# Quads two bodies earlier, indices decoded in PSUM, and the first value operands made inside the last key body

## The reference

```
q = (xb @ w_q).reshape(p, 8, 2, 128)
sc = jnp.einsum('thpc,hpnc->thpn', q, sub_keys)
s1, i1 = lax.top_k(sc[:, :, 0], 16);  s2, i2 = lax.top_k(sc[:, :, 1], 16)
cand = s1[..., :, None] + s2[..., None, :]
cand_idx = i1[..., :, None] * 128 + i2[..., None, :]
top_s, sel = lax.top_k(cand, 16)
eidx = take_along_axis(cand_idx, sel)
gate = softmax(top_s)
act = gelu(einsum('td,ted->te', xb, u[eidx])) * gate
out = einsum('te,ted->td', act, v[eidx])
```

## Time and profile before

| | |
|---|---|
| median of 3 runs | 2248.65 us (2247.8 to 2250.03) |
| profiled execution | 2248.29 us, span 2246.5 us |
| PE busy | 2128.1 us, 95% |
| DVE busy | 1473.0 us, 66% |
| ACT busy | 1312.9 us, 58% |
| POOL busy | 438.2 us, 20% |
| mean granted TensorE clock | 0.966 of 2.4 GHz |
| HBM | 336.66 MB read, 150 GB/s over the span |
| chain that ended last | PE 81%, DVE 8%, issue 4%, POOL 3%, ACT 2% |

### The profile page before, as it was taken

The page is one execution under the profiler, slowest core; times in us unless marked ns, Lnnn a source line. Parts: engine busy times, 40 slices in busy tenths (PEclk is TensorE's granted clock), DMA queues, the critical chain, the costliest instruction groups (busy, mean ns, idle before and its releaser), DMA issues.

```text
span 2246.5 us, 45241 instructions
## 1 busy us (share of the span) xinstructions
PE 2128.1 (95%) x14596; PEld 1927.4 (86%) x14596; DVE 1473.0 (66%) x2926; ACT 1312.9 (58%) x3097; POOL 438.2 (20%) x358
## 2 busy tenths in 40 slices
PE   7899899899999899999898998997999998999997
PEld 7889599899999788888787885997999997888886
DVE  5764247968878666666567533489687886666665
ACT  5530145479999755555564302553899996555554
POOL 0312007752222100000004020176522220000000
PEclk9999799999999999999999997998999999999999
DMA  5310244344444355555542102453444443555555
GB/s 222 113 57 1 94 150 171 144 153 168 157 161 168 131 187 194 198 187 192 182 183 94 57 1 94 169 176 124 169 165 155 166 158 141 189 195 194 188 196 186
DMA packets 47459, 338.77 MB, mean 151 GB/s; under 512 B 5648, under 2 KB 5776, under 8 KB 6928
## 3 DMA queue, kind: packets, MB, share of 16 engines
q1 hardware_dynamic: 47376, 337.73, 41.5%
HBM read 336.66 MB, written 1.05 MB: 150 GB/s over the span
## 4 chain that ended last, share of the span: by engine, by line
PE 81%; DVE 8%; issue 4%; POOL 3%; ACT 2%; DMA 2%; DVEq 0%; SPq 0%; POOLq 0%; PEldq 0%; ACTq 0%
PE ps L814 10%; PE ps L815 10%; PE ps L816 10%; PE ps L783 9%; PE ps L785 8%; PE ps L784 8%; POOL expert_lo L1826 3%; PE ps L686 3%; PE ps L407 2%; PE ps L409 2%; PE ps L408 2%; PE ps L550 2%; PE ps L563 1%; PE ps L562 1%; PE ps L793 1%
## 5 line engine op out<-in xcount | busy, mean ns | idle before, releaser
L783 PE MATMUL ps<-h_t_hi,expert_hi 128*128 128x256 f32 x2048 | 595.7, 291 | 27.3 <-DVE expert_lo L1656 22.1
L784 PE MATMUL ps<-h_t_lo,expert_hi 128*128 128x256 f32 x2048 | 582.8, 285 | 0.0
L785 PE MATMUL ps<-h_t_hi,expert_lo 128*128 128x256 f32 x2048 | 582.4, 284 | 0.0
L1826 POOL TENSOR_TENSOR expert_lo<-w_ring,expert_hi 128x512 fp32r<-128x512 f32 x220 | 338.1, 1544 | 763.9 <-ACT expert_hi L976 760.4
L783 PEld LDWEIGHTS ps<-h_t_hi,expert_hi 128*128 128x128 f32 x2048 | 396.0, 193 | 31.9 <-issue 13.3
L814 PE MATMUL ps<-expert_hi,act_hi 128*128 128x512 f32 x1024 | 400.5, 391 | 4.8 <-DVE act_lo L1664 4.8
L815 PE MATMUL ps<-expert_lo,act_hi 128*128 128x512 f32 x1024 | 400.1, 391 | 0.0
L816 PE MATMUL ps<-expert_hi,act_lo 128*128 128x512 f32 x1024 | 400.0, 391 | 0.0
L784 PEld LDWEIGHTS ps<-h_t_lo,expert_hi 128*128 128x128 f32 x2048 | 396.3, 194 | 0.0
L785 PEld LDWEIGHTS ps<-h_t_hi,expert_lo 128*128 128x128 f32 x2048 | 395.9, 193 | 0.0
L976 ACT CAST expert_hi<-w_ring 128x512 fp32r<-128x512 f32 x512 | 308.9, 615 | 141.9 <-PE ps L785 129.1
(11 more groups left out here) (293 smaller groups left out, 3359.5 us busy)
## 6 DMA issues: line engine op xcount, KB each, us to landing
w_ring<-u_t SPq DMA_DIRECT2D x128, 1024.0 KB, 4.8
w_ring<-v_t SPq DMA_DIRECT2D x128, 1024.0 KB, 4.8
w_ring<-w_in SPq DMA_DIRECT2D x32, 1024.0 KB, 4.9
w_ring<-w_q SPq DMA_DIRECT2D x16, 1024.0 KB, 4.9
w_ring<-w_out SPq DMA_DIRECT2D x8, 1024.0 KB, 4.8
big<-xconst SPq DMA_DIRECT2D x2, 1666.0 KB, 9.3
w_ring<-keys SPq DMA_DIRECT2D x2, 1024.0 KB, 4.8
big<-rows SPq DMA_DIRECT2D x2, 576.0 KB, 11.3
```

The lines of the kernel that those rows point to most:

```text
L783: pe.matmul(o, w_hi[:, c, :], HTH[:, d, :], start=d == 0, stop=False)
L784: pe.matmul(o, w_hi[:, c, :], HTL[:, d, :], start=False, stop=False)
L785: mm = pe.matmul(o, w_lo[:, c, :], HTH[:, d, :], start=False, stop=d == DC - 1)
L1826: pool.tensor_tensor(EL[:, m % 4, :], RING[:, m // 4, (m % 4) * 512:(m % 4 + 1) * 512], EH[:, m % 4, :].bitcast(F32), ALU.subtract).then_i ...
```

## The change

- QB goes from 12 to 10, FREE from 11 to 9 and EXP_BODY from 9 to 7. DVE has two lows a body in bodies 1 to 8, and the quads start in body 10. The slots of ones are made five a body in bodies 1 to 7.
- Body 30 has its three quads and prepares one more, body 31 has that one, and nothing stands between body 31 and the value product. In body 31 ACT and DVE make the first four splits of v and the first two of the activations where a body before makes those of the next body.
- The decode works on arrays of 16 x 16 for all 16 pairs of head and token tile at once. A key 128 x (start of the row in the table) + first index is picked by 15 comparisons and 15 predicated copies; from it come the first index (its low seven bits) and the column, which picks the second index in 15 more pairs. Positions and masks lie in PSUM banks 0 to 3 (DECODE), and a wait asks for all but the last instruction issued.
- Of 13 lows (17 before) that are threaded into the search some stand in other places.
- At the last level of `invert` the product with the upper half and its addition to TI are left out; nothing reads that half.

Cut to its core:

```diff
-N_BODY, EXP_BODY, FREE, QB = 32, 9, 11, 12
+N_BODY, EXP_BODY, FREE, QB = 32, 7, 9, 10
 N_QUAD = S // 4
-N_LOOPED = 3 * (N_BODY - QB)
+ONES = 5
...
+        DECODE = PS[:, 0:4, :].rearrange("p b n -> p (b n)").rearrange("p (m u n) -> p m u n", m=8, u=16)
...
-                            pe.matmul(PS[:, 4 + 2 * k, h * 64:(h + 1) * 64], TT[:, u, :], first, start=True, stop=True)
+                            if b < 64:
+                                pe.matmul(PS[:, 4 + 2 * k, h * 64:(h + 1) * 64], TT[:, u, :], first, start=True, stop=True)
...
-                with pe.Fori(QB, N_BODY) as j:
-                    u_and_quads(j)
-                for q in range(N_LOOPED, N_QUAD):
-                    quad(q % 3, q)
+                with pe.Fori(QB, N_BODY - 1) as j:
+                    u_and_quads(j, (1, 4, 6))
+                u_and_quads(N_BODY - 1, (1,))
...
                     if m < 8 or not last:
                         u_split(m % 8, j + m // 8, False)
+                    else:
+                        v_split(m - 8, 0, True)
+                        if m % 2 == 0:
+                            a_split((m - 8) // 2, 0, True)
...
                     if e == 0:
                         act.wait_ge(quad_out, 3 + N_QUAD)
+                else:
+                    if first and e == 2:
                         act.wait_ge(u_mul, 2 + 128 - LATE)
-                else:
                     act.wait_ge(v_done, 8 * j + 2 * e - 2)
...
-                    ones(bass.ds(LATE - 3 + 3 * j, 3), 3)
+                    ones(bass.ds(LATE - ONES + ONES * j, ONES), ONES)
...
-                for q in range(N_LOOPED + 2, N_QUAD):
-                    gate_rows(q % 3, q, 0, 8)
-                for m in range(4):
-                    v_split(m, 0, True)
-                for e in range(2):
-                    a_split(e, 0, True)
...
+                at = DECODE[:, 7, :, :]
+                dve.tensor_copy(PICK[:, :, :], ROWKEY[:, :, 0:1].broadcast_to([P, 16, 16]))
+                link(dve.tensor_copy(at, POS[:, :, :].bitcast(U32)))
...
+                def all_but(n):
+
+                    dve.wait_ge(dve_step, steps[0] - n)
+
+                def overwrite(dst, i, src):
+
+                    counted(dve.copy_predicated(dst[:, :, :], DECODE[:, i % 7, :, :].bitcast(U32), src.broadcast_to([P, 16, 16])))
+
+                for i in range(1, 17):
+                    if i < 16:
+                        counted(dve.tensor_scalar(DECODE[:, i % 7, :, :], at, float(ROW_AT[i]), None, ALU.is_ge))
+                    if i > 1:
+                        all_but(1 if i < 16 else 0)
+                        overwrite(PICK, i - 1, ROWKEY[:, :, i - 1:i])
+                    if i == 9:
+                        few_lows(1)
...
+                for i in range(1, 17):
+                    if i < 16:
+                        counted(dve.tensor_scalar(DECODE[:, i % 7, :, :], at, 128.0 * (i - 1), None, ALU.is_gt))
+                    if i > 1:
+                        all_but(1 if i < 16 else 0)
+                        overwrite(I2F, i - 1, x[:, :, 1, i - 1:i])
+                    if i in (6, 14):
+                        few_lows(1)
...
+                def next_lows(m):
+
+                    if not last:
+                        u_lows(m, j + 1)
+                    else:
+                        v_lows(m, 0)
+                        if m % 2 == 0:
+                            a_lows(m // 2, 0)
...
-                for q in range(N_LOOPED, N_QUAD):
-                    gated(q % 3, q, 128 - LATE)
-                    if q + 3 < N_QUAD:
-                        hots(q % 3, q + 3, False)
-                for m in range(2):
-                    v_lows(m, 0)
-                a_lows(0, 0)
-                for m in range(2, 8):
+                with dve.Fori(QB, N_BODY - 2) as j:
+                    u_and_gated(j, 3, 3, False)
+                u_and_gated(N_BODY - 2, 3, 1, False)
+                u_and_gated(N_BODY - 1, 1, 0, True)
+                for m in range(4, 8):
```

More of the change, by code:

```diff
@@ L795, in quad, with u_and_quads @@
                 mm.then_inc(quad_done, 1)
-            def u_and_quads(j):
-                q = 3 * (j - QB)
+            def u_and_quads(j, after):
                 for m in range(8):
                     u_half(m, j, False)
-                    if m in (1, 4, 6):
-                        i = (1, 4, 6).index(m)
-                        quad(i, q + i)
+                    if m in after:
+                        i = after.index(m)
+                        quad(i, 3 * (j - QB) + i)
             def v_half(m, j, first):
@@ L1011, in gate_rows, with u_and_gates @@
                     ins.then_inc(hot_gate, 1)
-            def u_and_gates(j, last):
+            def u_and_gates(j, quads, last):
                 q = 3 * (j - QB)
@@ L1023, in u_and_gates @@
                 u_gelu_late(0, j)
-                gate_rows(2, q + 2, 0, 6)
+                if quads:
+                    gate_rows(2, q + 2, 0, 6)
                 split(6)
@@ L1027, in u_and_gates @@
                 split(7)
-                gate_rows(2, q + 2, 6, 8)
-                gate_rows(0, q + 3, 0, 4)
+                if quads:
+                    gate_rows(2, q + 2, 6, 8)
+                    gate_rows(0, q + 3, 0, 4)
                 split(8)
@@ L1032, in u_and_gates @@
                 u_gelu_late(2, j)
-                gate_rows(0, q + 3, 4, 8)
-                gate_rows(1, q + 4, 0, 2)
+                if quads:
+                    gate_rows(0, q + 3, 4, 8)
+                if quads == 3:
+                    gate_rows(1, q + 4, 0, 2)
                 split(10)
@@ L1037, in u_and_gates @@
                 split(11)
-                gate_rows(1, q + 4, 2, 8)
+                if quads == 3:
+                    gate_rows(1, q + 4, 2, 8)
             def v_split(m, j, first):
@@ L1580, in topk @@
                         ins = dve.match_replace(SC2[:, u % 16, :], VAL[:, u, 0:8], SC[:, u, :], NEG)
-                        if u % 16 == (7 if t else 11):
+                        if t and u % 16 == 7:
                             few_lows(1)
@@ L1602, in topk @@
                     o += n
-                dve.tensor_copy(STEP1[:, :, 0:1], x[:, :, 0, 0:1])
-                dve.tensor_tensor(STEP1[:, :, 1:16], x[:, :, 0, 1:16], x[:, :, 0, 0:15], ALU.subtract)
+                rows = ROWC[:, 0, :].unsqueeze(1).broadcast_to([P, 16, 16])
+                dve.scalar_tensor_tensor(ROWKEY[:, :, :], rows, 128.0, x[:, :, 0, :], ALU.mult, ALU.add)
+                dve.tensor_copy(I2F[:, :, :], x[:, :, 1, 0:1].broadcast_to([P, 16, 16]))
                 link(dve.tensor_tensor(CAND[:, :, o:o + 8], v[:, :, 0, 8:16], v[:, :, 1, 0:1].broadcast_to([P, 16, 8]), ALU.add))
@@ L1685, in u_muls, with u_and_gated, quad_step, hot_step @@
                 dve.tensor_tensor(a, a, PS[:, 6 + e % 2, 0:S], ALU.mult).then_inc(u_mul, 1)
-            def u_and_gated(j, last):
+            def u_and_gated(j, quads, next_quads, last):
                 q, done = 3 * (j - QB), 4 * (j - QB)
+                def quad_step(i):
+                    if i < quads:
+                        gated(i, q + i, done + i)
+                def hot_step(i):
+                    if i < next_quads:
+                        hots(i, q + 3 + i, False)
+                def next_lows(m):
[5 more added lines that the diff above has]
+                            a_lows(m // 2, 0)
                 u_lows(4, j)
                 u_lows(5, j)
-                gated(0, q, done)
-                hots(0, q + 3, False)
+                quad_step(0)
+                hot_step(0)
                 u_lows(6, j)
-                u_muls(0, j, q + 1)
-                gated(1, q + 1, done + 1)
-                if not last:
-                    u_lows(0, j + 1)
-                hots(1, q + 4, False)
-                u_muls(1, j, q + 2)
-                if not last:
-                    u_lows(1, j + 1)
-                gated(2, q + 2, done + 2)
-                if not last:
-                    u_lows(2, j + 1)
-                hots(2, q + 5, False)
-                u_muls(2, j, q + 3)
-                u_muls(3, j, q + 3)
+                u_muls(0, j, q + min(1, quads))
+                quad_step(1)
+                next_lows(0)
+                hot_step(1)
+                u_muls(1, j, q + min(2, quads))
+                next_lows(1)
+                quad_step(2)
+                next_lows(2)
+                hot_step(2)
+                u_muls(2, j, q + quads)
+                if last:
+                    v_lows(3, 0)
+                u_muls(3, j, q + quads)
             norm_rows(0, HN)
```

71 lines of the change are left out of this document (33 added, 38 removed).

## The result

The changed kernel takes **2182.52 us** (median of 4 runs, 2180.91 to 2188.99) against 2248.70 for the kernel before: ratio 0.9711, 95% interval 0.9691 to 0.9731. The profiled execution took 2180.91 us, span 2179.1.

A forecast was written before the change was run, and what follows sets the result against it. PE, 95% busy, was taken as the bound, with VectorE bounding key bodies 5 to 9. Gain: 61.0 - 2 x 2.0 - 2 x 4.5 = 48.0, plus 5.3, is 53.3 us, giving 2195.4 us; range 2186 to 2212.

The forecast's parts named there:

- The stalls: Key product: PE pauses for late VectorE lows and the half-clock time behind them, 4.5 us a layer.
- the transposes: Key bodies 8 to 10: six transposes and the first masks keep their time above PE's floor, 2.0 us a layer.
- the prediction's last paragraph: Signs to check: PE pauses above 0.5 us, one before half 30 and one or two between halves 46 and 58.
- half 30: Key product: the VectorE low due for this half body of matmuls comes 1.5 us late, after index searches and candidate sums.
- low 12: Last VectorE low threaded into the search, behind the decode's instructions: 1.3 us late.
- the 1.7 for a half-clock period: Key product: one period of PE at half clock behind the pauses, 1.7 us of loss a layer.
- The decode: VectorE's decode of positions: 60 instructions at 0.36 us, 2.5 us of small ones and four lows of 0.6, 26.5 us.
- the first rival: VectorE's small decode instructions don't overlap, 0.46 us each: 15 us more in all, 2210.4 us; 12%.
- the slower one: Decode instructions on PSUM cost so much that VectorE sets bodies 5 to 9; gain gone at 0.86 us each; 3%.
- Quads and seam: Quads from body 10 at 13.02 us a body; value product directly behind the key product, nothing above the floor, up to 1 us.
- The second rival: Seam from key to value product isn't closed: 4.5 us a layer, 9 more, 2204.4 us; 12%.
- The inverse: Last level of the inverse on PE: dropped matmuls save 2.67 us a layer, 5.3 for both; bounds 0 and 8.7.

The follow-up runs named there:

- decode_sbuf: Changed kernel with the decode's masks and positions in SBUF instead of PSUM: 2207.45 us in one execution.
- seam_undone: Changed kernel with the first four splits of v and first two of the activations back behind body 31: 2208.09 us in one execution.
- lows_placed: Changed kernel with VectorE's lows threaded into the search where each falls in its window, fourteen instead of thirteen: 2186.54 us in one execution.

## Why the prediction was wrong

**The stalls: near in sum, partly by luck.** Of the 7.6 us a layer above the floor, bodies 3 to 7 have 5.3 (forecast 4.5) and bodies 9 and 10, with the transposes, 2.2 (2.0). The pauses stand where the prediction's last paragraph looked for them: before half 30, and at halves 46 and 54 in the decode. Their sizes are others. Body 3 loses 0.8 us where 1.5 were forecast, and bodies 5 and 6 lose 3.3 where the sum had 1.3 for low 12, which isn't late. Body 7 loses 1.1, most of it by a pause that had no term, behind ScalarE's gelu (the last row), and the 1.7 for a half-clock period are 0.

```profile
372.58 0.38 PE L784 MATMUL ps<-h_t_hi,expert_hi 128*128 128x256 f32 x1 [0.56 <-DVE expert_lo L1686]
397.23 0.38 PE L784 MATMUL ps<-h_t_hi,expert_hi 128*128 128x256 f32 x1 [1.25 <-DVE expert_lo L1686]
410.57 0.38 PE L784 MATMUL ps<-h_t_hi,expert_hi 128*128 128x256 f32 x1 [1.57 <-DVE expert_lo L1686]
420.31 0.39 PE L784 MATMUL ps<-h_t_hi,expert_hi 128*128 128x256 f32 x1 [0.68 <-ACT big L980]
```

The half-clock period that was added didn't come; none of the pauses is as long as the 3.98 us of the earlier trace rows.

**The decode: 29.4 us for 26.5.** The 60 instructions and what lies between them run from 389.89 to 417.62, 27.7 us; with the two small ones ahead, which the 26.5 included, it is 29.4 from 388.17:

```profile
390.56 0.45 DVE L1648 COPY_PREDICATED h_t<-ps,big 128x256 f32<-128x256 uint32 x1
390.90 0.43 DVE L1652 TENSOR_SCALAR ps<-ps 128x256 f32<-128x256 f32 x1
391.24 0.45 DVE L1648 COPY_PREDICATED h_t<-ps,big 128x256 f32<-128x256 uint32 x1
...
395.66 1.43 DVE L1686 TENSOR_TENSOR expert_lo<-w_ring,expert_hi 128x512 fp32r<-128x512 f32 x1
...
403.19 1.29 DVE L1661 CAST h_t<-h_t 128x256 int32<-128x256 f32 x1
```

A start every 0.34 us (0.36 taken, 0.33 the lower bound), though each lasts 0.44: they overlap by 0.1 us, and the first rival falls, with it the slower one, which needed 0.86. Four lows took 4.1 us instead of 2.4, and the seven small ones 4.9 instead of 2.5, among them a copy of 1.35 and the cast of 1.29: pieces above 1 us, which the prediction excluded. The likely reason is the one that decode_sbuf shows, VectorE waiting for POOL. The sum had priced them as if VectorE worked alone. POOL's lows went from 2.57 us to 1.30:

```profile
401.09 1.30 POOL L1869 TENSOR_TENSOR expert_lo<-w_ring,expert_hi 128x512 fp32r<-128x512 f32 x1 [2.85 <-ACT expert_hi L975]
```

**Quads and seam: right.** Bodies from 11 on take 13.02 us; the first value matmul follows the last key body's last half without a pause, and value body 1 comes 10.91 us later. The second rival falls, and seam_undone shows its price: 5.3 us a layer, 4.5 forecast.

**The inverse: right in its place, wrong behind it.** Its last level takes 2.79 us in 24 passes. Before, it took 5.47 in 48, so it is 2.68 shorter, forecast 2.67:

```profile
205.14 2.79 PE L564 MATMUL ps<-big 128*128 128x64 f32 x24
```

The step that failed is the term's bound: "bounds 0, and 8.7 if a half-clock period behind it gets shorter too". One short period was allowed for. There were 20 us in each layer, both could go, and the mixers gave 21.4 us, 12.7 beyond the bound. The prediction gives the clock by stretches from 338 us on only; the row 225 to 245 at 0.50, with PE busy throughout, lies ahead of them. A forecast with it in view would have had two cases, stretch stays and stretch goes, 16 us apart: 2195 and 2179, and the runs of the changed kernel lie near both and between (2180.6 to 2199.7).

What stays open is why fewer matmuls ahead make the better form more frequent. On PE the edit does no more there than start the chunks 2.7 us earlier; the traces don't show the chip's reason.

## What to carry to other kernels

Read the granted clock over the whole span before pricing an edit, not in the stretches that it touches, and treat a half-clock stretch in which the engine never pauses as a price that may go or come with a small edit, or between two executions of one program. Where a stage has rows of small matmuls and wide ones that may go anywhere, try the wide ones among them: here the order of two a layer was worth 18.8 us to the kernel before, and took the spread between runs from 13 to 19 us down to 4 to 6. And put the operands of small VectorE instructions into PSUM when POOL works beside them: in SBUF the decode cost 6.6 us a layer more. Where they stay in SBUF, a moved instruction can newly fall beside one of POOL's, so place by a fresh trace.

## What was unexpected of the hardware

- The same program takes two forms, 8 to 9 us apart in a layer, and both can occur in one execution (lows_placed: 168.9 us in layer 0, 176.6 in layer 1). Two traces of the changed kernel agree to 0.07 us from 202.8 to 222.8 us and part there at the clock. The Trainium skill (TensorE: Matmul & The Clock Gate, "Part 1: The HAM clock gate (the "warmup" mystery)") says that the window over which the clock gate judges activity is free-running and isn't reset when a kernel starts, so that one kernel differs between runs; that the two traces part where the kernel is the same agrees with it.
- TensorE fell to 1.2 GHz without pausing: busy 20.00 of 20 us at 0.50, behind passes of 64 columns. The same page's table has the low level as the default and behind an idle stretch. Here the measurement decides: PE's last pause before that fall, 0.96 us, had ended 13.8 us earlier.
- A VectorE instruction of 0.28 us with its operands in SBUF takes 1.38 beside a low of POOL, and with them in PSUM 0.42 to 0.45 throughout the changed kernel's decode. In SBUF the candidate sums take 2.3, 4.6 or 5.6 us, by how many of them fall beside one.
